# Expert weights loaded matrix by matrix in 16 KB runs, and the token gather cut into two halves of the slots

## The chip, the cores and the metric

The kernel runs on one core of one Trainium2 chip. The metric is the time of one execution on the device in microseconds (us), the median of several runs. A profile is one such execution, recorded by the hardware profiler. The work is spread over TensorE (PE in the rows, its weight loads PEld), VectorE (DVE), ScalarE (ACT), GpSimd (POOL) and SyncE (SP), which here only issues DMAs; 16 DMA engines carry them out.

## The reference

One decoder layer over 256 tokens of width 2048, all in float32. It ends in a mixture of 32 experts with 256 hidden columns each; every token uses 2 experts of one group.

```python
def hybrid_layer(x, ...):
    h = rms_norm(x, norm1_g)
    z = h @ w_in                                  # 2048 x 11272
    ...                                           # conv, mLSTM heads, attention heads, gates
    y = sigmoid(gm) * (hm @ w_branch_m) + sigmoid(ga) * (ha @ w_branch_a)
    x = x + y @ w_out
    x = x + hier_moe(rms_norm(x, norm2_g), ...)
    return x                                      # then a final RMSNorm

def hier_moe(h, w_grp, b_grp, w_exp, b_exp, w1, w3, w2):
    ...                                           # top group, top 2 experts in it, weights `combine`
    hid = silu(einsum('td,edf->tef', t, w1)) * einsum('td,edf->tef', t, w3)
    hid = hid * combine[..., None]
    return einsum('tef,efd->td', hid, w2)
```

Each expert has three matrices of 2 MiB (w1, w3, w2), so the experts read 201.3 MB; everything before them reads about 133 MB.

## The kernel before, in words

**Dense stages.** All matrices up to `w_out` stream through four buffers `wraw` of 1 MiB, are split by ACT and DVE into a rounded part and a rest (`wsplit`) and multiplied on PE. This part is the same in both kernels, but for one copy.

**From the router to the first expert (the seam).** After the last unit of `w_out` PE sums the router logits. DVE picks the two experts of every token, gives each of the 512 (token, expert) pairs a slot sorted by expert, and writes `sel`, a 0/1 matrix from the tokens to the 512 slots (L1613, L1616). PE gathers (L1081): for each of the 16 chunks of the width it multiplies the token rows, as a rounded part `x2hi` and a rest `x2lo`, by `sel`: four matmuls with 512 moving columns, their weights read with a step of 16 elements. A 17th product (L1078) gives each slot the RMS factor of its token. ACT and DVE in turn copy the chunks from PSUM to `xg`.

**Pairs of experts.** The experts are worked off two at a time, 16 pairs, with 64 slots each (an `If` chooses this form when no expert has more than 64 tokens; this run takes it). For each expert of a pair DVE multiplies the slots' columns of `xg` by the RMS factors into `xe`; PE multiplies `xe` by w1 and w3 side by side (`hidden`, L1094); ACT takes the sigmoid and DVE the products (`silu`); PE turns the result (`turn`). Then come the rows of w2 for both experts (`rows`, L1123), ACT and DVE split the sums into `ys_hi` and `ys_lo`, and PE spreads them to the tokens (`scatter`, L1139 and L1140, in eight groups of 512 columns), which DVE adds to `x2` (L1697). The scatter of a pair lies between the matmuls of the next.

**Buffers and loads.** `w13_a` and `w13_b` hold w1 and w3 of the even and the odd expert of one pair (4 MiB each). `w2s` has two slots of two buffers of 2 MiB, so the rows of two pairs. SP issues the loads in program order and waits before each until PE has used what the buffer held:

```python
def load_hidden(b, e, kh):                    # w1 and w3, one half of the contraction
    ks = slice(kh * HALF_K, (kh + 1) * HALF_K)
    for w, w_v in enumerate((w1_v, w3_v)):
        sp.dma_start(w13[b][:, kh, w], w_v[:, e, ks]).then_inc(w13_loaded[b][kh], 16)
```

Such a load has 8 KB in one run on each partition; a load of w2 has two runs of 4 KB. Before the gather ends, both `w13` and three of the four w2 buffers are filled; the fourth (`w2_a0`) shares its memory with `x2lo` and is loaded after the gather.

**The end.** After the last pair's rows the eight groups are scattered, added, squared on ACT and multiplied by `final_g` on DVE (L1742); then come the sum of squares, its root (POOL), the scaling and the store.

Of the kernel before, what the change touches and what calls it, by code (L numbers as in the profile page):

```python
# [14 lines left out]
F32 = mybir.dt.float32  # L15
F32R = mybir.dt.float32r
# [36 lines left out]
WARM_ROUTE, WARM_SELECT = 20, 12  # L53
# [21 lines left out]
GROUPS_OUT = TT * D // 512  # L75
REV = 384
# [55 lines left out]
def layer(nc, x, norm1_g, w_in, conv_w, if_bias, mnorm_g, w_branch_m, w_branch_a, w_out, rel_bias,  # L132
          norm2_g, w_grp, b_grp, w_exp, b_exp, w1, w3, w2, final_g, onehot, out):
    ctx = ExitStack()
    with ctx:
# [11 lines left out]
        def sem(name):  # L147
# [31 lines left out]
        x2hi = sb("x2hi", [P, TT, D], F32R, at=AT_QK + 16 * KB)  # L179
# [99 lines left out]
        hid = sb("hid", [P, P])  # L279
        sg = sb("sg", [P, P])  # L280
        spare = sb("spare", [P, 1])
        slot_w = sb("slot_w", [P, 1])
        mix = sb("mix", [P, TT, P])
        assert place["at"] <= AT_W2

        slot_of = sb("slot_of", [P, T], F32R, at=AT_ONES_R)
        hidT = sb("hidT", [P, 2, P], at=AT_IOTA_S)
# [40 lines left out]
        gexp_go, gexp_done, mk_ready, rank_summed, sel_ready, xg_summed, xg_act, xg_dve, tab_ready = (  # L328
            sem(n) for n in ("group_exp_go", "group_exp_done", "chosen_ready", "rank_summed",
                             "selection_ready", "gathered", "gathered_even", "gathered_odd",  # L330
                             "table_ready"))
        w13_loaded = [[sem(f"w13{b}_{kh}_loaded") for kh in ("upper", "lower")] for b in "ab"]
        w2_loaded = [[sem(f"w2_loaded{slot}_{side}") for side in ("left", "right")] for slot in range(2)]
        xe_ready, h_summed, sg_ready, hid_ready, hid_turned, hidT_ready, y_summed, ys_ready = (
            sem(n) for n in ("xe_ready", "hidden_summed", "hidden_sigmoid", "hid_ready", "hid_turned",
                             "hidT_ready", "ye_summed", "ye_ready"))
        upper_used = sem("upper_chunks_used")
# [16 lines left out]
        w2_v = w2.rearrange("e (j p) n -> p e j n", p=P)  # L354
# [9 lines left out]
        gathers = [*range(12), None, *range(12, DC)]  # L364
# [27 lines left out]
        def _(sp):  # L392
# [1385 lines left out]
```

## Time and profile before

| | before |
|---|---|
| time, median of 3 runs | 1253.61 us (1253.21 to 1253.68) |
| the profiled execution: time | 1249.93 us |
| its span | 1248.2 us |
| PE busy | 1193.2 us (96%) |
| DVE, ACT busy | 707.1 us (57%), 408.1 us (33%) |
| read from memory | 333.93 MB |
| core's mean DMA rate | 269 GB/s over the span |

The time is the device's for a whole execution, the span is from the first to the last recorded instruction, so the two differ by 1.7 us in the profiled execution. A busy PE isn't a PE at its peak, since matmuls overlap in the records: a high share says only that something is always in flight. The DMA share and the GB/s of a stretch say more about the last third of this kernel.

### The profile page before, as it was taken

What the parts mean: (1) busy time and instruction counts of PE and PEld (TensorE: products, weight loads), DVE (VectorE), ACT (ScalarE), POOL (GpSimd) and SP (SyncE); (2) the same over time, 40 slices, a digit from 0 to 9 for tenths busy, and PEclk for the clock granted to TensorE, in tenths of its full rate; (3) what the DMA queues carried; (4) which work ended last, traced back from release to release, by engine and by line L of the source; (5) the groups of instructions that cost most, each with busy time, mean ns of one, the idle gap of its engine ahead of it and who ended that gap; (6) DMA issues with size and microseconds to landing.
All of it is one profiled execution on the core that took longest, in us unless ns stands there. A gap on an engine that the chain in (4) does not pass through costs nothing.

```text
span 1248.2 us, 19400 instructions
## 1 busy us (share of the span) xinstructions
PE 1193.2 (96%) x7310; PEld 895.4 (72%) x7310; DVE 707.1 (57%) x1009; ACT 408.1 (33%) x464; POOL 38.3 (3%) x54
## 2 busy tenths in 40 slices
PE   8999999999999999999999998999999998999995
PEld 8888888888888888888888887555555544444442
DVE  5777555554666766667885555344454444444445
ACT  5444433334344354444344542111112111111113
POOL 1000000001002022000000000000000000000000
PEclk9999999999999999999999999999999999999997
DMA  8665655555555455556765674999999999999993
GB/s 286 191 188 183 186 184 182 189 180 176 183 169 170 136 166 168 168 168 192 248 177 172 236 304 149 366 417 424 425 426 425 425 425 426 424 425 425 425 424 151
DMA packets 170150, 336.57 MB, mean 270 GB/s; under 512 B 12144, under 2 KB 136192, under 8 KB 153088
## 3 DMA queue, kind: packets, MB, share of 16 engines
q1 hardware_dynamic: 165536, 335.69, 73.0%
q10 hardware_dynamic: 4576, 0.37, 0.3%
q8 instruction: 25, 0.41, 0.1%
q14 instruction: 13, 0.11, 0.0%
HBM read 333.93 MB, written 2.11 MB: 269 GB/s over the span
## 4 chain that ended last, share of the span: by engine, by line
PE 57%; issue 40%; DVE 1%; DMA 1%; ACT 0%; POOL 0%; ACTq 0%; POOLq 0%; SPq 0%; DVEq 0%
PE ps L836 19%; PE ps L865 11%; PE ps L838 10%; PE ps L867 5%; PE ps L1003 5%; PE ps L1004 2%; PE ps L823 1%; DMA xin<-in_x_dram 1%; PE ps L972 0%; PE ps L1023 0%; DVE wsplit L1188 0%; PE ps L852 0%; ACT wsplit L585 0%; PE ps L854 0%; PE ps L853 0%
## 5 line engine op out<-in xcount | busy, mean ns | idle before, releaser
L1188 DVE TENSOR_TENSOR wsplit<-wraw,wsplit 128x2048 fp32r<-128x2048 f32 x120 | 277.1, 2309 | 181.2 <-ACT wsplit L585 180.3
L836 PE MATMUL ps<-act_split,wsplit 128*128 128x512 f32 x1024 | 362.4, 399 | 0.0
L585 ACT ACTIVATE wsplit<-wraw 128x2048 fp32r<-128x2048 f32 x120 | 230.1, 1917 | 383.4 <-PE ps L838 203.4
L838 PE MATMUL ps<-act_split,wsplit 128*128 128x256 f32 x1024 | 286.8, 280 | 0.0
L836 PEld LDWEIGHTS ps<-act_split,wsplit 128*128 128x128 f32 x1024 | 192.2, 188 | 48.0 <-issue 1.8
L865 PE MATMUL ps<-wsplit,act_split 128*128 128x512 f32 x608 | 216.2, 400 | 2.2 <-DVE wsplit L1188 2.1
L838 PEld LDWEIGHTS ps<-act_split,wsplit 128*128 128x128 f32 x1024 | 193.3, 189 | 0.2
L867 PE MATMUL ps<-wsplit,act_split 128*128 128x256 f32 x608 | 170.3, 280 | 0.0
L865 PEld LDWEIGHTS ps<-wsplit,act_split 128*128 128x128 f32 x608 | 114.2, 188 | 30.9 <-issue 2.7
L1094 PE MATMUL ps<-w_a,xe 128*64 128x256 f32 x1024 | 115.4, 381 | 13.6 <-DMA w_a<-in_w_dram 11.4
L1672 DVE TENSOR_TENSOR hid<-sg,ps 128x128 f32<-128x128 f32 x32 | 9.2, 288 | 204.8 <-ACT sg L778 204.8
L1094 PEld LDWEIGHTS ps<-w_a,xe 128*64 128x64 f32 x1024 | 72.6, 137 | 61.3 <-DMA w_a<-in_w_dram 20.2
L1094 PE MATMUL ps<-w_b,xe 128*64 128x256 f32 x1024 | 115.7, 381 | 0.0
L867 PEld LDWEIGHTS ps<-wsplit,act_split 128*128 128x128 f32 x608 | 114.8, 189 | 0.0
L1123 PE MATMUL ps<-w_a,hidT 128*64 128x512 f32 x256 | 113.3, 595 | 0.4 <-ACT hidT L781 0.4
L1123 PE MATMUL ps<-w_b,hidT 128*64 128x512 f32 x256 | 113.3, 595 | 0.0
L1094 PEld LDWEIGHTS ps<-w_b,xe 128*64 128x64 f32 x1024 | 71.4, 137 | 41.6 <-issue 4.3
L1697 DVE TENSOR_TENSOR x<-x,ps 128x512 f32<-128x512 f32 x128 | 84.9, 683 | 8.9 <-PE ps L1140 6.9
L1003 PE MATMUL ps<-br_split,wsplit 128*128 128x512 f32 x256 | 88.8, 394 | 0.0
L1123 PEld LDWEIGHTS ps<-w_a,hidT 128*64 128x64 f32 x256 | 33.7, 137 | 70.0 <-issue 69.5
L1139 PE MATMUL ps<-ys_hi,slot_of 128*128 128x512 f32 x128 | 61.5, 480 | 18.5 <-DVE x L1697 18.5
L778 ACT ACTIVATE sg<-ps 128x128 f32<-128x128 f32 x32 | 8.9, 278 | 197.3 <-PE ps L1094 197.3
(288 smaller groups left out, 1148.3 us busy)
## 6 DMA issues: line engine op xcount, KB each, us to landing
w_a<-in_w_dram SPq DMA_DIRECT2D x96, 1024.0 KB, 18.4
w_b<-in_w_dram SPq DMA_DIRECT2D x96, 1024.0 KB, 21.5
wraw<-in_w_in_dram SPq DMA_DIRECT2D x88, 1024.0 KB, 5.0
wraw<-in_w_out_dram SPq DMA_DIRECT2D x16, 1024.0 KB, 5.2
wraw<-in_w_branch_m_dram SPq DMA_DIRECT2D x8, 1024.0 KB, 5.1
wraw<-in_w_branch_a_dram SPq DMA_DIRECT2D x8, 1024.0 KB, 5.1
xin<-in_x_dram SPq DMA_DIRECT2D x2, 1024.0 KB, 6.1
x<-in_x_dram SPq DMA_DIRECT2D x1, 2048.0 KB, 9.3
```

The source lines that it names most:

```text
L585: act.activation(wsplit[:, q % 2, :, 0], wraw[:, q % RAW], ACT.Copy).then_inc(rounded, 1)
L836: pe.matmul(banks[b], w[:, k, 0, b * P:(b + 1) * P], a, start=first and k == 0, stop=False)
L838: last = pe.matmul(banks[b][:, 0:T], w[:, k, 1, b * P:(b + 1) * P], a[:, 0], start=False, stop=last_half and k == HALF_K - 1)
L865: pe.matmul(banks[t], a[:, 0, t * P:(t + 1) * P], w[:, k], start=first and k == 0, stop=False)
L867: last = pe.matmul(banks[t][:, 0:UNIT], a[:, 1, t * P:(t + 1) * P], w[:, k, 0], start=False, stop=last_half and k == HALF_K - 1)
L1003: pe.matmul(bank, w[:, k, 0, b * P:(b + 1) * P], a, start=k == 0, stop=False)
L1004: last = pe.matmul(bank[:, 0:T], w[:, k, 1, b * P:(b + 1) * P], a[:, 0], start=False, stop=k == HALF_K - 1)
L1094: last = pe.matmul(ps[f * SLOTS:(f + 1) * SLOTS, 0, 0:2 * P].rearrange("p (w f) -> p w f", w=2), xe[:, b, k], w13[b][:, k // HALF_K, :, k ...
L1123: last = pe.matmul(ps[b * SLOTS:(b + 1) * SLOTS, 2 + n], hidT[:, b, f * SLOTS:(f + 1) * SLOTS], w2s[slot][b][:, f, n * 512:(n + 1) * 512], ...
L1139: pe.matmul(ps[:, 6 + g % 2], to_tokens, ys_hi[:, n * 512:(n + 1) * 512], start=True, stop=False)
L1188: dve.tensor_tensor(wsplit[:, q % 2, :, 1], wraw[:, q % RAW], wsplit[:, q % 2, :, 0].bitcast(F32), ALU.subtract).then_inc(split, 1)
L1697: dve.tensor_tensor(cols, cols, ps[:, 6 + g % 2], ALU.add).then_inc(added, 1)
```

## The change

Four things change, all from the seam on.

1. **Loads.** w1 and w3 of an expert are loaded as whole matrices (2 MiB, one run of 16 KB on each partition), w1 of both experts once the pair before has used w1, then w3 likewise. w2 is cut as `(p j)` in place of `(j p)`, so that it too has one run of 16 KB. The first pairs are loaded in parts of 1 MiB (8 KB runs), the last pair's w2 in pieces of 512 columns. `w2_a0` moves to memory that is free early and is loaded ahead of the gather.
2. **Order in a pair.** PE multiplies by w1 for both experts, then by w3 for both, in four parts; one `turn` for the pair; two scatter groups of the pair before stand behind each part. The RMS factor and the routing weight are applied to the hidden values, so `xe` is a plain copy.
3. **Gather.** It runs over the first 256 slots (`side` 0) and then over the other 256 (`side` 1), each with 16 chunks of four matmuls with 256 moving columns. Eleven chunks of side 0 stand ahead of the first pair, the rest between its parts. ACT alone copies to `xg`. `x2` is made again from `x2hi` + `x2lo` after the gather.
4. **Tail.** The last pair's rows, rounding, scatter, adds and squares go piece by piece; POOL multiplies six groups by `final_g`, DVE two.

```diff
-            def load_hidden(b, e, kh):
-                ks = slice(kh * HALF_K, (kh + 1) * HALF_K)
-                for w, w_v in enumerate((w1_v, w3_v)):
-                    sp.dma_start(w13[b][:, kh, w], w_v[:, e, ks]).then_inc(w13_loaded[b][kh], 16)
+                def next_hidden(i):
+                    for w, w_v in enumerate((w1_v, w3_v)):
+                        parts_done(i, 2 * w + 1)
+                        for b in range(2):
+                            sp.dma_start(w13[b][:, w], w_v[:, ds(i * 2 + b, 1)]).then_inc(w13_loaded[w][0], 16)
+                def next_rows(i, slot):
+                    rows_free(i)
+                    for b in range(2):
+                        load_rows(slot, b, ds(i * 2 + b, 1))
...
-        w2_v = w2.rearrange("e (j p) n -> p e j n", p=P)
+        w2_v = w2.rearrange("e (p j) n -> p e j n", p=P)
...
+            def gather(side, first, end):
+                pe.wait_ge(sel_ready, side + 1)
+                for c in range(first, end):
+                    n = side * DC + c
+                    if n >= 5:
+                        pe.wait_ge(xg_out, n - 4)
+                    for t in range(TT):
+                        for k, part in enumerate(parts):
+                            last = pe.matmul(ps[:, 3 + n % 5, 0:SIDE], part[:, t, c], sel[:, t, side * SIDE:(side + 1) * SIDE],
+                                             start=t == 0 and k == 0, stop=t == TT - 1 and k == 1)
+                    last.then_inc(xg_summed, 1)
+            gather(0, 0, AHEAD)
...
+                for part in range(PARTS):
+                    w, h = divmod(part, 2)
...
+                    for k in range(h * PART_K, (h + 1) * PART_K):
+                        for b in range(2):
+                            last = pe.matmul(ps[b * SLOTS:(b + 1) * SLOTS, 2 * w, 0:FF], operands[b][:, k], w13[b][:, w, k],
+                                             start=k == 0, stop=k == DC - 1)
+                    last.then_inc(h_parts, 1)
...
+                hidden(0, 0, (xg[:, :, 0:SLOTS], xe_first), [[lambda: gather(0, AHEAD, DC)], [lambda: gather(1, 0, 6)],
+                                                             [lambda: gather(1, 6, 12)], [lambda: gather(1, 12, DC)]])
+                turn(0)
+                pe.wait_ge(xg_out, 2 * DC)
+                rows(0, 0, 0)
...
+                    hidden(i, i, xe, [[lambda: scatter(i - 1, half, (0, 1))], [lambda: scatter(i - 1, half, (2, 3))],
+                                      [lambda: scatter(i - 1, half, (4, 5))], [lambda: scatter(i - 1, half, (6, 7))]])
+                    turn(i)
```

Where DVE makes `sel`, this stood in the kernel before (engine DVE; `table`, `rank` and `pos` are the slot counts, `ps` is PSUM):

```order
L1602 COPY table<-ps 128x32
L1603 SCALAR_TENSOR_TENSOR table<-ones,ps 128x31
L1605 COPY rank<-ps 128x64
L1607 TENSOR_TENSOR pos<-rank,table 128x64
L1609 TENSOR_TENSOR rt<-oh,pos 128x64 x2
L1611 TENSOR_REDUCE stat<-rt 128x4
L1613 TENSOR_SCALAR sel<-iota_s,stat 128x512 x2
L1616 SCALAR_TENSOR_TENSOR sel<-iota_s,stat,sel 128x512 x2
```

And this stands there now, on the same engine:

```order
L1718 SCALAR_TENSOR_TENSOR table<-ones,ps 128x31
L1721 TENSOR_TENSOR pos<-ps,table 128x64
L1723 TENSOR_TENSOR rt<-oh,pos 128x64 x2
L1725 TENSOR_REDUCE stat<-rt 128x4
L1731 TENSOR_SCALAR sel<-iota_s,stat 128x256 x2
L1735 SCALAR_TENSOR_TENSOR sel<-iota_s,stat,sel 128x256 x2
L1740 COPY rank<-ps 128x64
L1741 COPY table<-ps 128x32
```

Two small copies moved behind `sel`, and `sel` is made for 256 slots at first; the other 256 come after the first pair's tokens were copied.

On PE, the end of the gather and the first pair stood like this before (two matmuls of the last chunk, the branch into the pair-wise form, then the first pair):

```order
L1081 MATMUL ps<-sel,x2hi 128x512
L1081 MATMUL ps<-sel,x2lo 128x512
L369 TENSOR_LOAD most_i
L369 ISA x2
L370 COMPARE_AND_BRANCH
L1094 MATMUL ps<-w_a,xe 64x256 x32
L1112 MATMUL ps<-ident,hid 128x128
L1094 MATMUL ps<-w_b,xe 64x256 x32
L1109 MATMUL ps<-ident,mix 128x128 x2
```

Now, at the end of the first pair's first part, PE's rows are these (the last two of 16 matmuls of the part, the turn of `mix`, and the first two matmuls of the gather's next five chunks):

```order
L1186 MATMUL ps<-w_a,xg 64x256
L1186 MATMUL ps<-w_b,xe_first 64x256
L1167 MATMUL ps<-ident,mix 128x128 x2
L1155 MATMUL ps<-sel,x2hi 128x256
L1155 MATMUL ps<-sel,x2lo 128x256
```

A gather matmul is half as wide and there are 128 of them in place of 64; 44 stand ahead of the first pair, 20, 24, 24 and 16 behind its four parts, and all of them stand ahead of the pair's rows.

On SP, one turn of the loop loaded this for a pair before (`w_a` and `w_b` are the buffers of the even and the odd expert, ISA rows are waits and register work):

```order
L448 DMA w_a<-in_w_dram 128x2048 x2
L480 REGISTER_ALU
L448 ISA
L448 DMA w_a<-in_w_dram 128x2048 x2
L448 ISA
L448 DMA w_b<-in_w_dram 128x2048 x2
L480 REGISTER_ALU
L448 ISA
L448 DMA w_b<-in_w_dram 128x2048 x2
L489 REGISTER_ALU
L454 DMA w_a_61<-in_w_dram 128x2x1024
L454 DMA w_b_62<-in_w_dram 128x2x1024
```

And now:

```order
L492 DMA w_a<-in_w_dram 128x4096
L492 ISA
L492 DMA w_b<-in_w_dram 128x4096
L485 REGISTER_ALU
L492 DMA w_a<-in_w_dram 128x4096
L492 DMA w_b<-in_w_dram 128x4096
L464 ISA
L464 DMA w_a_63<-in_w_dram 128x4096
L464 ISA
L464 DMA w_b_64<-in_w_dram 128x4096
```

Six loads of 2 MiB take the place of twelve of 1 MiB; SP waits three times a pair, each wait ahead of 4 MiB, where it waited five times.

## Rows read from the trace of the kernel before

**Rows 1.** The page's slices: DMA share in tenths, GB/s, 40 slices of 31.2 us

```profile
DMA  8665655555555455556765674999999999999993
GB/s 286 191 188 183 186 184 182 189 180 176 183 169 170 136 166 168 168 168 192 248 177 172 236 304 149 366 417 424 425 426 425 425 425 426 424 425 425 425 424 151
```

**Rows 2.** Windows: length, busy us (x count) by engine, PE clock, DMA share, GB/s

```profile
757.00:774.00 17.00, 16.10 (x65) 14.88 (x64) 7.88 (x19) 6.12 (x9) 0.00 (x0) 1.00 0.17 67
774.00:782.00 8.00, 6.75 (x63) 4.51 (x64) 3.23 (x6) 1.49 (x2) 0.00 (x0) 1.00 0.91 298
803.00:806.00 3.00, 3.00 (x30) 2.01 (x28) 0.00 (x0) 0.00 (x0) 0.00 (x0) 1.00 0.54 137
850.00:1000.00 150.00, 144.07 (x990) 78.23 (x986) 69.28 (x119) 28.12 (x45) 0.00 (x0) 1.00 1.02 425
1222.00:1223.00 1.00, 1.00 (x6) 0.29 (x4) 0.00 (x0) 0.00 (x0) 0.00 (x0) 1.00 0.68 287
```

**Rows 3.** Windows: w2 loads (4 KB runs), then w1 and w3 (8 KB runs)

```profile
1001.50:1011.30 9.80, 9.32 (x73) 5.58 (x72) 2.45 (x5) 0.55 (x2) 0.00 (x0) 1.00 1.01 418
1011.50:1031.00 19.50, 17.39 (x109) 8.29 (x107) 10.10 (x17) 4.27 (x6) 0.00 (x0) 1.00 1.02 428
```

**Rows 4.** Timeline of the seam: start, length, engine, line, what, count

```profile
753.47 0.88 DVE L1613 TENSOR_SCALAR sel<-iota_s,stat 128x512 fp32r<-128x512 f32 x2
754.39 1.41 DVE L1616 SCALAR_TENSOR_TENSOR sel<-iota_s,stat,sel 128x512 fp32r<-128x512 f32 x2
...
759.60 0.30 PEld L1081 LDWEIGHTS ps<-sel,x2hi 128*128 128x128 f32 x1
759.84 0.30 PEld L1081 LDWEIGHTS ps<-sel,x2lo 128*128 128x128 f32 x1
...
772.71 0.39 PE L1081 MATMUL ps<-sel,x2lo 128*128 128x512 f32 x1
...
775.25 7.13 PE L1094 MATMUL ps<-w_a,xe 128*64 128x256 f32 x64 [2.15 <-DVE xe L1658]
...
792.65 0.64 PE L1123 MATMUL ps<-w_a,hidT 128*64 128x512 f32 x1 [0.37 <-ACT hidT L781]
...
799.57 7.08 PE L1094 MATMUL ps<-w_a,xe 128*64 128x256 f32 x64
...
803.40 4.32 SPq L448 DMA_DIRECT2D w_a<-in_w_dram  x4
```

**Rows 5.** Timeline of the last dense unit: weight loads without a step

```profile
738.70 0.19 PEld L852 LDWEIGHTS ps<-wsplit,act_split 128*128 128x128 f32 x1
738.82 0.19 PEld L853 LDWEIGHTS ps<-wsplit,act_split 128*128 128x128 f32 x1
```

**Rows 6.** SP's DMA issues, the first load of two pairs that follow each other

```profile
830.79 4.25 SPq L448 DMA_DIRECT2D w_a<-in_w_dram  x4
...
858.18 4.24 SPq L448 DMA_DIRECT2D w_a<-in_w_dram  x4
```

**Rows 7.** Timeline: two scatter groups, and the turn ahead of the rows

```profile
1206.27 0.50 PE L1139 MATMUL ps<-ys_hi,slot_of 128*128 128x512 f32 x1
...
1207.07 0.40 PE L1140 MATMUL ps<-ys_lo_left,slot_of 128*128 128x512 f32 x1
...
791.96 0.33 PE L1112 MATMUL ps<-ident,hid 128*128 128x128 f32 x1 [0.65 <-DVE hid L1673]
```

**Rows 8.** The tail: timeline rows, then groups of instructions (count, busy us, mean ns)

```profile
1219.96 0.64 PE L1123 MATMUL ps<-w_a,hidT 128*64 128x512 f32 x1
...
1239.04 0.15 DVE L1747 TENSOR_REDUCE stat<-sq 128x2 f32<-128x8 f32 x1
...
L1697 DVE TENSOR_TENSOR x<-x,ps 128x512 f32<-128x512 f32 x128 | 84.9, 683 | 8.9 <-PE ps L1140 6.9
L786 ACT ACTIVATE ys_hi<-ps,slot_w 128x1024 fp32r<-128x1024 f32 x32 | 35.7, 1114 | 108.4 <-PE ps L1123 108.4
L794 ACT ACTIVATE fin<-x 128x512 f32<-128x512 f32 x8 | 5.0, 630 | 4.8 <-DVE x L1697 4.8
```

More of the change, by code:

```diff
@@ L1065, in _ @@
             last.then_inc(rank_summed, 1)
+            pe.wait_ge(rms_diag_ready, 1)
+            for t in range(TT):
+                last = pe.matmul(ps[:, 2, t * P:(t + 1) * P], ones[:], rms_diag[:, t], start=True, stop=True)
+            last.then_inc(rms_summed, 1)
             for n in range(WARM_SELECT):
@@ new lines, in turn, with rows @@
+            def turn(s):
+                pe.wait_ge(hid_ready, s + 2)
+                pe.wait_ge(hidT_ready, s + 1)
+                pe.wait_ge(slots_ready, s + 2)
+                for f in range(FC):
+                    last = pe.transpose(ps[:, 1, f * P:(f + 1) * P], hid[:, f * P:(f + 1) * P], ident[:])
+                last.then_inc(hid_turned, 1)
+            def rows(load_no, s, slot, ns=range(4)):
+                pe.wait_ge(hidT_ready, s + 2)
+                pe.wait_ge(ys_ready, s * 2 + 1)
+                if load_no is not None:
+                    pe.wait_ge(w2_loaded[slot], load_no * 32 + 32)
+                for n in ns:
+                    if load_no is None:
+                        pe.wait_ge(w2_last[n], 32)
@@ new lines, in experts, with pair @@
+                copy_rms_row()
+                second_tokens(0)
+                make_mix(0, 0, 0)
+                select(1)
+                second_tokens(1)
+                dve.memset(xg[:, :, PAIRS:], 0.0)
+                slots(0, 0)
+                gate(0)
+                up(0)
+                make_x2()
+                dve.wait_ge(xg_out, 2 * DC)
+                copy_tokens(starts_of(1, 0), 1)
+                make_mix(1, 0, 1)
+                def pair(i, half):
+                    ys_split(i - 1)
+                    slots(i, half, (i - 1) * GROUPS_OUT + 1)
+                    add(i - 1, (0, 1, 2, 3))
+                    gate(i)
+                    add(i - 1, (4, 5))
+                    up(i)
+                    add(i - 1, (6, 7))
@@ new lines, in experts @@
+                with steps_x.loop(0, N_PAIRS // 2 - 1, 4) as j:
+                    for n in (1, 2):
+                        i = j * 2 + n
+                        pair(i, n % 2)
+                        copy_tokens(starts_of(i + 1, 0), i + 1)
+                        make_mix(i + 1, 0, i + 1)
+                pair(LAST, 1)
+                for n in range(4):
+                    ys_split_part(LAST * 2 + (n + 1), n, n + 1)
+                    tail_add((2 * n, 2 * n + 1))
+            by_most(dve, experts)
```

515 lines of the change are left out of this document (282 added, 233 removed).

## The prediction

> **What bounds the kernel now.** I read the page's slices first. In the dense stages the DMA engines are busy half to two thirds of the time; from the 27th slice on they are busy throughout at 424 to 426 GB/s, up to the last slice [rows 1]. The stretch from 850 to 1000 us says it at one glance: share 1.02, 425 GB/s, PE's clock at its full 1.00 [rows 2]. So the pairs of experts are paced by the weights' arrival, not by PE. Then I looked for the edges of that stretch. Ahead of it is a hole: from 757 to 774 us the engines are busy 0.17 of the time, 774 to 782 runs at 298 GB/s, and at 803 to 806 there is a second, small hole (0.54, 137 GB/s) [rows 2]. At its end the stream stops in the slice 1222 to 1223, two thirds full, so at about 1223.1 [rows 2]; what comes behind is the tail, 25.1 us up to the span's end at 1248.2.
>
> The first hole's reason is room. All buffers but one are full, and SP may load again only when PE has used something: the gather ends at 772.71 + 0.39, the first pair's matmuls start at 775.25, its rows at 792.65, and the second pair starts at 799.57; the load that opens the unbroken stream is issued at 803.40 [rows 4]. At that point both experts' matrices of pairs 0 and 1, 12 of the 96 matrices of 2.097 MB, have been loaded. What is left is 84 of them and `final_g`, 176.2 + 1.05 = 177.2 MB. At 425 GB/s that takes 417.0 us; counted from 806, where the flow is back, it gives 1223.0, which is where the stream ends [rows 2]. So the end is: the moment at which the stream can start, plus bytes over rate, plus the tail. The change touches all three.
>
> **The start of the stream.** In the new order, SP has room for the first pair's parts during the seam: w1 and w3 of pair 1, the same 4 matrices as before. The next load, w2 of pair 2, waits for the rows of pair 0 to be done, and the bytes behind that point are again 84 matrices and `final_g`. So the new start of the stream is the end of the first pair's rows, where it was 803.40.
>
> - Making `sel`: DVE took 0.88 us for two instructions of 512 columns and 1.41 us for two more [rows 4]. With half the columns, and a fixed part that I put at 0.06 us in each (estimate, as the small DVE instructions of about 0.2 us bound it), they take 0.50 and 0.77, 1.0 less; a copy moved behind gives 0.1 more: **-1.1 us**.
> - The gather: before, from the end of `sel` at 755.80 to 773.10, it was 64 matmuls, 0.24 us apart (759.60 and 759.84), and the RMS product, some 17 us [rows 4]. Now it is 128 matmuls with half the moving columns. No row shows one. The bounds: a 256-column matmul whose weights lie side by side goes every 0.12 us (738.70 and 738.82) [rows 5], so 128 x 0.12 = 15.4 us; or the spacing stays at the 0.235 us of the 512-column ones, 30.1 us. What decides is the weight load: with the step of 16 elements it takes 0.30 us, without it 0.19 [rows 4, 5]. If the 0.11 us more is time in which the load occupies its path, the spacing can't go below 0.12 + 0.11 = 0.23, and halving the columns halves nothing. I take 0.23: 29.5 us, **+12.5 us**.
> - The waits: between the gather's end and the first rows there were 792.65 - 773.10 = 19.55 us, of which 2 x 7.13 = 14.3 were matmuls of `hidden` [rows 4] (the second expert's group is as long) and 5.3 were waits for `xe` and for the two silu chains. Now the silu of the gate lies under the gather, and what is left is the turn of `mix` (0.4), the wait of the second part for the 16th chunk's copy and the token copy (0.9), and a turn with the copy of `hidT` ahead of the rows (0.69 before, 791.96 to 792.65 [rows 7, 4], for two transposes 0.85). With 0.5 for the branch, which is no longer under a wait, 2.65: **-2.7 us**. The rows stay at 6.9 us.
>
> Together +8.7: the rows of pair 0 end at 799.57 + 8.7 = 808.3, and the stream's first load is issued at 808.4, **5.0 us later than 803.40**. `make_x2` (two DVE instructions) and the token copies of pair 1 lie under the rows; without that cover they would cost up to 5 us. The extra 2 MiB that is loaded ahead finds room between 740 and 760 us and buys nothing by itself, since the w2 buffer it fills was already refilled before 803 in the kernel before.
>
> A rule bears on the gather. The Trainium skill, page "SBUF — State Buffer", section "Specifications (TRN2)", says that an engine's reads run at full bandwidth only with at least two hits in a 16-byte line. Four-byte elements with a step of 16 never give that, and the trace agrees: 0.30 against 0.19 us. By that rule the gather takes the 29.5 us; without it 15.4.
>
> **Bytes over rate.** The two kinds of load can be told apart in the trace: while w2 comes (4 KB runs) 418 GB/s, while w1 and w3 come (8 KB runs) 428 [rows 3]. Each of 16 engines then needs 156.8 ns for 4 KB and 306.2 ns for 8 KB: 149.4 ns for each 4 KB, and 7.4 ns that come with the run whatever its length. A 16 KB run should take 306.2 + 298.8 = 605 ns, which is 433 GB/s. The lower bound for the rate is the 428 of the 8 KB runs, or the 425 of today if w2's other layout explains nothing. 82 of the 84 matrices, 172.0 MB, take 397.2 us at 433 and took 404.6 at 425: **-7.4 us**. The last two w2 come in runs of 2 KB: 82.1 ns each, 399 GB/s, 10.5 us for 4.19 MB where it was 9.9: **+0.6 us**.
>
> The Trainium skill, page "DMA: Bandwidth & Descriptors", section "Bandwidth", gives 435 GB/s as the ceiling of the fabric and about three cycles on top of each packet. By an estimate from that page the 16 KB runs reach 432, so 6.5 us would be gained in place of 7.4.
>
> So the stream ends at 1223.1 + 5.0 - 7.4 + 0.6 = 1221.3.
>
> **The tail.** Before, rows to sum of squares took 1239.04 - 1219.96 = 19.1 us [rows 8], and the rows started 3.1 us ahead of the stream's end. Now the last w3 is in flight until 1221.3 - 2.5 - 10.5 (`final_g` and w2 stand behind it) + 1.5 for its arrival to be seen (estimate: the last pair's PE work before stood about as far behind the stream) = 1209.8. PE then does two parts of 3.6 us, two scatter pairs of 1.05 (1206.27 to 1207.07 and one spacing of 0.24 more [rows 7]), the turn and the wait for `hidT` (1.2): rows start at 1220.4. The rest goes piece by piece. PE: 1.7 us of rows per piece, so 6.9 in all, and three scatter pairs between them, 3.2. Behind the last piece: rounding 0.6 (half of 1114 ns, and a little), split 0.7, scatter 1.1, two adds 1.4, the last square 0.8 [rows 8], and 0.7 for signals between engines: 15.4 us, to 1235.8; and DVE's two products by `final_g` may push it by 0.5. Sum of squares at 1236.3, and 9.2 us from there to the end as before (1239.04 to 1248.2): 1245.5. The tail is 24.2 us behind the stream, against 25.1; with PE's clock, which I don't know there, I take **-1.3 us** with 1 us of doubt either way. POOL's products for six groups are at most 2 us each and end before the last square.
>
> **The sum**: 5.0 - 7.4 + 0.6 - 1.3 = -3.1 us. The span goes from 1248.2 to 1245.1, the profiled execution from 1249.93 to 1246.8; the median of the runs lies 3.7 above the profiled execution, which I carry over: **1250.5 us**. A difference of 0.2% (2.5 us) is about the least that a measurement of this kernel can tell from none, so this is barely a gain. Its own range is 1246 to 1256: the stream's start may be off by 2 us, the rate by 3, the tail by 1.5.
>
> **Rivals.**
>
> *The step in the weights costs nothing with fewer columns.* The 128 matmuls then go at 0.12 us: 14.1 us less than in my sum, everything behind follows, since the stream is unbroken. Time 1236. For it: the 0.30 us might be delay and not occupancy, for the loads overlap at 0.24 us spacing. Against it: the loads without a step keep 0.19 us at either spacing, so the length of a record does look like service. Chance 0.16.
>
> *The runs' length gives nothing.* Then the rate stays at 425 and the 7.4 us are missing: 1258; at 428, the present best, 4.6 us are missing: 1255. For it: the two rates come from windows of 10 and 20 us and differ by only 2.4%, and w2's pieces differ from the others also in where they lie in memory. Against it: the mean of 425 over 150 us [rows 2] is what one third at 418 and two thirds at 428 give, so the difference is not noise of these windows. Chance 0.14, most of it slower.
>
> *PE becomes the bound (the other side).* Loads are freed in steps of 4 MiB now. PE's own pace before was 27.4 us a pair, while it still had a lead of data (830.79 to 858.18) [rows 6]. I count 4 x 3.67 + 6.9 + 4 x 1.05 + 0.3 + 0.85 = 27.0 for the new order: the scatter in pairs meets free banks, but `hidT` is waited for in the open. The stream needs 12.58 MB / 433 = 29.1 us a pair. PE starts pair 1 at 808.3 and must be at the second half of pair 15 at 1209.8; that is 14 periods and 9.8 us, so it decides above 28.0 us a pair, with 14 us for each further 1 us. At 28.5 the time is 1257.5. Against it: the margin of 1 us; DVE has some 14 us of work in a pair, and each of SP's waits ends 3 to 10 us before the stream would run dry. Chance 0.13, nearly all slower.
>
> What is left, 0.05, is a tail or a seam that is shorter in some way I don't see (0.04), or longer.
>
> **How the numbers follow.** Mine 0.52 (0.32 faster by over 0.2%, 0.18 within, 0.02 slower), the free step 0.16 (faster), no gain in rate 0.14 (0.04 within, 0.10 slower), PE as the bound 0.13 (0.02, 0.11), the rest 0.05 (0.04 faster, 0.01 slower): faster 0.52, same 0.24, slower 0.24. The range takes in 1236 of the first rival and 1258 of the second.
>
> **What would show it.** In the changed kernel: gather matmuls with 256 columns at a spacing near 0.23 us (or 0.12, then the first rival); the rows of pair 0 ending near 808; slices of the pairs at 432 to 434 GB/s; PE waiting for the DMA at w1 and w3 in the later pairs, and pairs 29 us apart; the stream ending near 1221 and the sum of squares 15 us behind it. The prediction is wrong if the stream runs dry between pairs, if the rate stays at 425, or if the gather is cheap.

## The result, and the profile after

The changed kernel takes 1257.89 us (median of 5 runs, 1255.55 to 1259.0), the kernel before 1253.21 (5 runs on the same chip): ratio 1.0034, 95% interval 1.002 to 1.0048. It is slower by 0.34%, where 1250.5 us and a small gain were forecast. The profiled execution took 1255.84 us, its span 1254.0.

The page's slices answer to [rows 1]:

```profile
GB/s 285 191 185 187 194 174 194 173 198 171 176 164 166 156 162 164 166 163 191 266 176 171 253 351 187 221 428 430 432 431 432 432 430 432 430 432 432 408 390 115
```

The weights now come at 430 to 432 GB/s, up to the 37th slice. Then it falls to 408 and 390.

The timeline of the seam (start, length, engine, line, what), beside [rows 4]:

```profile
753.24 0.62 DVE L1731 TENSOR_SCALAR sel<-iota_s,stat 128x256 fp32r<-128x256 f32 x2
753.89 0.88 DVE L1735 SCALAR_TENSOR_TENSOR sel<-iota_s,stat,sel 128x256 fp32r<-128x256 f32 x2
...
755.31 0.31 PEld L1155 LDWEIGHTS ps<-sel,x2hi 128*128 128x128 f32 x1
755.44 0.38 PE L1155 MATMUL ps<-sel,x2hi 128*128 128x256 f32 x1
755.53 0.31 PEld L1155 LDWEIGHTS ps<-sel,x2lo 128*128 128x128 f32 x1
755.66 0.38 PE L1155 MATMUL ps<-sel,x2lo 128*128 128x256 f32 x1
...
801.12 0.61 PE L1213 MATMUL ps<-w_a,hidT 128*64 128x512 f32 x1 [0.67 <-ACT xg L806]
808.01 0.38 PE L1186 MATMUL ps<-w_a,xe_a 128*64 128x256 f32 x1
808.24 0.33 SPq L464 DMA_DIRECT2D w_a<-in_w_dram  x1
```

The gather's matmuls of 256 columns are 0.22 us apart, pair 1 starts at 808.01, and SP issues the load that opens the stream at 808.24 (forecast 808.4). The same timeline has the gather's 128 matmuls in five stretches that fill 29.4 us of PE (forecast 29.5), with 2.4 us of waits between the gather's start and the rows (forecast 2.65).

The timeline of PE at the heads of two steady pairs and of the last two, with the wait ahead of each in brackets; SP's issue of w1 of pair 15; the third part of pair 15 (the first that needs its w3, 1218.62); the last rows; and DVE's sum of squares:

```profile
1065.22 0.43 PE L1186 MATMUL ps<-w_a,xe_a 128*64 128x256 f32 x1 [1.87 <-DMA w_b<-in_w_dram]
...
1094.35 0.43 PE L1186 MATMUL ps<-w_a,xe_a 128*64 128x256 f32 x1 [1.89 <-DMA w_b<-in_w_dram]
...
1181.91 0.43 PE L1186 MATMUL ps<-w_a,xe_a 128*64 128x256 f32 x1 [1.90 <-DMA w_b<-in_w_dram]
...
1190.53 0.33 SPq L492 DMA_DIRECT2D w_a<-in_w_dram  x1
...
1209.01 0.38 PE L1186 MATMUL ps<-w_a,xe_a 128*64 128x256 f32 x1
...
1218.62 0.43 PE L1186 MATMUL ps<-w_a,xe_a 128*64 128x256 f32 x1
...
1228.87 0.64 PE L1213 MATMUL ps<-w_a,hidT 128*64 128x512 f32 x1 [0.47 <-ACT hidT L821]
...
1244.32 0.15 DVE L1922 TENSOR_REDUCE stat<-sq 128x2 f32<-128x8 f32 x1
```

A steady pair takes 29.13 us (1065.22 to 1094.35), and once in it PE waits 1.9 us for w1. The last such wait is at 1181.91, for w1 of pair 14. From there on PE waits for no load, w3 of pair 15 included: pair 14 takes 27.1 us, pair 15 another 19.9 up to its rows. The last rows start at 1228.87, 8.5 us later than forecast [rows 8 for before].

The windows there say that the stream was no longer the one that set the pace (the last three numbers are PE's granted clock, where 1.00 is its full level, the DMA share and GB/s):

```profile
1180.00:1188.00 8.00, 6.10 (x51) 3.88 (x52) 3.10 (x8) 1.02 (x1) 0.00 (x0) 1.00 1.02 436
1188.00:1194.00 6.00, 6.00 (x50) 3.69 (x48) 2.35 (x5) 0.47 (x1) 0.00 (x0) 1.00 0.69 240
1194.00:1202.00 8.00, 7.33 (x54) 4.41 (x50) 3.22 (x5) 0.38 (x1) 0.00 (x0) 1.00 1.01 426
1202.00:1206.00 4.00, 3.90 (x18) 1.39 (x20) 2.19 (x6) 0.15 (x1) 0.00 (x0) 1.00 0.97 307
1206.00:1226.00 20.00, 20.00 (x150) 11.65 (x148) 7.87 (x14) 2.38 (x3) 0.00 (x0) 1.00 1.01 406
```

At 1188 to 1194 the engines run at 240 GB/s while PE is busy in all 6 us. SP issues w1 of pair 15 at 1190.53, when PE has used w1 of pair 14; here w2 of pair 15 stood in between before. A second, smaller hole follows at 1202 to 1206 (307 GB/s), ahead of w3 of pair 15, for the same reason.

### The profile page after: what moved, and what is told of

It is laid out like the page before. It is cut to its first block, busy times and chain, and to the rows that moved or that the text cites. A ratio compares the mean times of both kernels' runs of the same rounds, so it can differ in the third digit from the quotient of the medians.

```text
span 1254.0 us, 19144 instructions
## 1 busy us (share of the span) xinstructions
PE 1199.7 (96%) x7366; PEld 909.2 (73%) x7366; DVE 693.0 (55%) x1019; ACT 383.6 (31%) x419; POOL 45.8 (4%) x60
## 4 chain that ended last, share of the span: by engine, by line
PE 77%; DMA 18%; DVE 2%; issue 1%; ACT 1%; SPq 0%; POOL 0%; ACTq 0%; POOLq 0%; DVEq 0%
PE ps L904 19%; DMA w_b<-in_w_dram 17%; PE ps L1186 12%; PE ps L933 11%; PE ps L906 10%; PE ps L935 5%; PE ps L1071 5%; PE ps L1213 3%; PE ps L1072 2%; PE ps L1155 2%; PE ps L1222 1%; PE ps L1223 1%; DMA xin<-in_x_dram 1%; PE ps L891 1%; PE ps L1091 1%
## 5 line engine op out<-in xcount | busy, mean ns | idle before, releaser
L1186 PE MATMUL ps<-w_a,xe_a 128*64 128x256 f32 x960 | 219.8, 382 | 19.9 <-DMA w_b<-in_w_dram 19.7
L1186 PE MATMUL ps<-w_b,xe_b 128*64 128x256 f32 x960 | 219.8, 382 | 0.0
L1186 PEld LDWEIGHTS ps<-w_a,xe_a 128*64 128x64 f32 x960 | 126.9, 137 | 109.0 <-DMA w_b<-in_w_dram 34.3
L1186 PEld LDWEIGHTS ps<-w_b,xe_b 128*64 128x64 f32 x960 | 126.9, 137 | 0.0
L1837 DVE TENSOR_TENSOR x<-x,ps 128x512 f32<-128x512 f32 x120 | 77.1, 684 | 84.9 <-PE ps L1223 81.6
L1072 PE MATMUL ps<-br_split,wsplit 128*128 128x256 f32 x256 | 70.9, 277 | 0.0
L827 ACT ACTIVATE ys_hi<-ps 128x1024 fp32r<-128x1024 f32 (+1 forms) x34 | 33.1, 973 | 98.7 <-PE ps L1213 98.7
L1222 PE MATMUL ps<-ys_hi,slot_of 128*128 128x512 f32 x128 | 56.9, 445 | 1.5 <-DVE ys_lo_right L1822 1.5
```

What stands on the lines that cost most here:

```text
L1072: last = pe.matmul(bank[:, 0:T], w[:, k, 1, b * P:(b + 1) * P], a[:, 0], start=False, stop=k == HALF_K - 1)
L1186: last = pe.matmul(ps[b * SLOTS:(b + 1) * SLOTS, 2 * w, 0:FF], operands[b][:, k], w13[b][:, w, k], start=k == 0, stop=k == DC - 1)
L1222: pe.matmul(ps[:, bank], to_tokens, ys_hi[:, n * 512:(n + 1) * 512], start=True, stop=False)
L1837: dve.tensor_tensor(cols, cols, ps[:, 6 + g % 2], ALU.add).then_inc(added, 1)
```

## The experiments

The profiled executions differ by up to 6 us in when `sel` starts (751.6 to 757.7 us), although all kernels but the one before share nearly all of the code up to there; the changed kernel's own two differ by 1.7 us. So I read each run in three stretches: from the first row of `sel` to the head of pair 1 (the seam), from there to the first row of the last pair's `rows` (the stream), and from there to the sum of squares (the tail).

| kernel | `sel` starts | seam | stream | tail | time or ratio |
|---|---|---|---|---|---|
| before | 753.47 | 46.1 | 420.4 | 19.1 | 1 |
| changed | 753.24 | 54.8 | 420.9 | 15.5 | 1.0034 |
| changed, forecast | | 54.8 | 412.1 | 15.9 | |
| one_gather | 756.91 | 43.0 | 421.5 | 15.5 | 0.9922 |
| w2_lag_early | 755.67 | 54.8 | 418.0 | 15.5 | 1.0019 |
| no_last_w2 | 755.07 | 54.8 | 421.0 | 15.5 | 1257.68 us |
| pad_last | 754.23 | 54.8 | 424.4 | 15.5 | 1260.31 us |
| one_gather_lag_early | 755.40 | 43.0 | 417.0 | 15.5 | 0.9921 |
| gather_side_by_side | 755.51 | 41.6 | 420.7 | 15.4 | 1244.67 us |
| short_runs | 753.37 | 56.4 | 422.1 | 15.5 | 1258.81 us |
| pad_every_pair | 757.71 | 54.8 | 425.2 | 15.5 | 1264.65 us |
| changed_again | 751.55 | 54.8 | 420.5 | 15.5 | 1.0036 |
| w2_in_place | 755.43 | 54.8 | 425.3 | 15.5 | 1.0063 |

The three stretches are the same to 0.4 us in both profiles of the changed kernel, so differences of a microsecond count in them, even where one execution's time could not tell them. One thing has to be taken out first: in some executions the granted clock falls to its lower level (0.50 in the rows, 1.2 GHz in place of 2.4) for 3.4 to 6.8 us in the midst of the work. Where PE sets the pace, 3.4 us of it cost 1.7. The seam of short_runs and the streams of w2_lag_early and w2_in_place have one such stretch each that PE has to pay for. From the sum of squares to the span's end the changed kernel takes 9.7 us, 0.5 more than before; that lies in the store, and I did not follow it up.

The forecast missed in the stream alone, by 8.8 us.

My theory after the result: behind the arrival of w1 of pair 14 stand 47 us of PE's own work, and the stream, with w2 of pair 15 moved to its end, no longer covers them. The rivals: the stream ended too late, by its holes and the pieces of 2 KB runs; or PE bound the whole way.

**no_last_w2.** The changed kernel without the loads of the last pair's w2 and the waits for them (the rows of pair 15 are made with what is in the buffer):

```
                 cols = slice(n * 512, (n + 1) * 512)
-                for b in range(2):
-                    sp.dma_start(w2s[1][b][:, :, cols], w2_v[:, 2 * LAST + b, :, cols]).then_inc(w2_last[n], 16)
...
-                    if load_no is None:
-                        pe.wait_ge(w2_last[n], 32)
```

> The changed kernel without the loads of the last pair's w2 and the waits for them; the last pair uses the rows of pair 13 that are in the buffer, so this part of the result is left out. The stream ends 10 us earlier. Theory A (PE gates the end): the last rows start at 1228 to 1229 as before and the span stays within 1 us of 1254.0. Rival B (the stream's end decides): the span falls by 8 to 10 us.

The stream stretch is 421.0 against 420.9, although 4.2 MB less are loaded at its end. PE's rows at the last head and the last rows:

```profile
1210.97 0.38 PE L1184 MATMUL ps<-w_a,xe_a 128*64 128x256 f32 x1
...
1230.81 0.64 PE L1209 MATMUL ps<-w_a,hidT 128*64 128x512 f32 x1 [0.47 <-ACT hidT L819]
```

Again 19.84 us between them. The span, 1256.0, is 1 us outside what I had expected; `sel` starts 1.8 us later here. The stream's late end costs nothing; PE sets the end.

**pad_last.** 16 matmuls of `ident` more, behind the third part of the last pair, into a bank that the rows overwrite:

```
+                def pad():
+                    for _ in range(16):
+                        pe.matmul(ps[:, 5, 0:P], ident[:], ident[:], start=True, stop=True)
...
-                                        [lambda: scatter(LAST - 1, 0, (4, 5))], [lambda: scatter(LAST - 1, 0, (6, 7))]])
+                                        [lambda: scatter(LAST - 1, 0, (4, 5)), pad], [lambda: scatter(LAST - 1, 0, (6, 7))]])
```

> The changed kernel with 16 matmuls of the identity (32 records of 0.12 us, 3.8 us) added behind the third part of the last pair. Theory A (PE gates the end): the span grows by 3.8 us, all of it. Rival B (PE waits for the last w2 pieces or w3 there): the span grows by 0 to 1 us.

```profile
1210.01 0.38 PE L1186 MATMUL ps<-w_a,xe_a 128*64 128x256 f32 x1
...
1233.41 0.64 PE L1213 MATMUL ps<-w_a,hidT 128*64 128x512 f32 x1 [0.47 <-ACT hidT L821]
```

23.4 in place of 19.9 us, 3.5 more. The added matmuls run from 1224.25 to 1227.9, so all of their time is paid (it is 3.5 and not the 3.8 that I had counted). Nothing else is waited for in the last pair.

**pad_every_pair.** The same with 8 matmuls, in pairs 1 to 15 (in `hidden_and_scatter`).

> 8 more matmuls of 128 columns behind the third part of every pair from 1 to 15, 1.7 us by the run with 16 of them. Theory (PE has slack of 1.9 us in each pair from 4 to 13, and none in 14 and 15): the last rows start 3.4 us later counted from the start of pair 1, 424.3, and the time is about 1261 us; the wait for w_b in the steady pairs falls from 1.9 us to 0.2. Rival (the prediction's third rival, PE decides from 28.0 us a pair on, 14 us for each further 1 us): PE's own pace is now 28.7, so 0.7 x 14 = 10 us are to be paid, 1268 us; if PE bound every pair, 15 x 1.7 = 25 us.

```profile
1158.00 0.43 PE L1186 MATMUL ps<-w_a,xe_a 128*64 128x256 f32 x1
...
1187.22 0.43 PE L1186 MATMUL ps<-w_a,xe_a 128*64 128x256 f32 x1
1216.07 0.38 PE L1186 MATMUL ps<-w_a,xe_a 128*64 128x256 f32 x1
...
1237.68 0.64 PE L1213 MATMUL ps<-w_a,hidT 128*64 128x512 f32 x1 [0.47 <-ACT hidT L821]
```

The pairs are 28.8 us apart (1187.22 to 1216.07) but for the one before, 29.2 (1158.00 to 1187.22), and at no head does PE wait for a load longer than 0.1 us, where I had expected 0.2. Yet pair 14 starts 374.7 us behind pair 1, against 373.9 without the padding. So in the first 13 pairs 13 x 1.75 us were swallowed but for 0.8, and the last two paid 1.8 each: +4.3, where I expected 3.4 and the rival 10 or 25. The time of 1264.65 us also holds a `sel` that started 4.5 us late. The limit from which PE sets the start of pair 14 is 373.9 / 13 = 28.8 us a pair; PE's own pace is 27.0. PE did not bind the whole way.

**w2_in_place.** The last w2 stands again between w3 of pair 14 and w1 of pair 15, `final_g` at the end:

```
                 next_hidden(LAST - 1)
-                next_hidden(LAST)
                 rows_free(LAST)
                 for n in range(4):
-                    if n == 0 and chunks == 1:
-                        load_final_g(chunks)
...
+                next_hidden(LAST)
+                load_final_g(chunks)
```

> The last pair's w2 is loaded in its old place, between w3 of pair 14 and w1 of pair 15; final_g comes last. Theory (behind w1 of pair 14 stand 27.1 us of PE for pair 14 and 20 for pair 15, and without the last w2 only 3 matrices of 9.7 us in the stream): with w2 back there PE waits for w1 and then w3 of pair 15, and the last w3 sets the end. The stream has no hole near 1190 and ends near 1223; w3 is there near 1221.5, and two parts, two scatter pairs and the turn (10.4 us) bring the last rows to 1232, 3 us later than 1228.9, 424 us behind the start of pair 1: about 1260 us. So w2 at the end is worth 3 us of the 10.8 that the prediction booked for it. Rival (the late place costs by the hole in the stream, which then ends later): without the hole everything ends 2.7 us earlier, 1255 us.

```profile
1184.14 0.43 PE L1183 MATMUL ps<-w_a,xe_a 128*64 128x256 f32 x1 [1.91 <-DMA w_b<-in_w_dram]
...
1213.96 0.40 PE L1183 MATMUL ps<-w_a,xe_a 128*64 128x256 f32 x1 [2.49 <-DMA w_b<-in_w_dram]
...
1235.53 0.64 PE L1210 MATMUL ps<-w_a,hidT 128*64 128x512 f32 x1 [0.47 <-ACT hidT L818]
```

PE waits again for w1 of pair 15 (2.5 us). From that head to the rows it takes 21.6 us in place of 19.9, but not by a wait for w3, as I had expected: the only waits there are the 2.5 us at the head and the 0.47 for `hidT`. It is the clock. Just behind the wait the granted clock falls to its lower level, and the matmuls of the first part go every 0.43 us in place of 0.22:

```profile
1214.90:1218.30 3.40, 3.40 (x20) 2.38 (x18) 0.00 (x0) 0.00 (x0) 0.00 (x0) 0.50 1.00 424
```

The stretch is 425.3, 4.4 longer than with w2 last; 1.7 of them are the clock, 2.7 the order (3 expected). And the time is 1261.5 us, ratio 1.0063 [1.0047, 1.008] against 1.0036 [1.0023, 1.0048] for the changed kernel on the same chip. The hole at 1188 is nearly gone (401 GB/s), and it is no faster: the hole wasn't the cause. Moving w2 to the end is right, and worth some 3 us in the stretch (4 in the medians, 1261.5 and 1257.36), not the 10.5 by which it was to bring w3 forward.

**changed_again**, beside it.

> The changed kernel again, on the same chip as the next one: 1256 to 1259 us, the last rows 421 us behind the start of pair 1.

1257.36 us (6 runs), stream stretch 420.5.

**w2_lag_early.** If PE's 47 us behind w1 of pair 14 set the end, w1 must come earlier in the stream, and something else later. Up to pair 10 w2 is loaded a pair ahead of its w1; here w2 of pair 11 and of those that follow goes behind w1 and w3 of the same pair:

```
-                with sp.Fori(0, N_PAIRS // 2 - 2) as j:
+                with sp.Fori(0, N_PAIRS // 2 - 4) as j:
...
-                next_hidden(LAST - 1)
+                next_hidden(LAST - 5)
+                for i in range(LAST - 4, LAST):
+                    next_hidden(i)
+                    next_rows(i, i % 2)
                 next_hidden(LAST)
```

> The changed kernel with w2 of a pair moved behind its w1 and w3 from pair 11 on, and not for the last pair alone. Theory A (PE gates the end: from the arrival of w1 of pair 14 it has 27.1 us of pair 14 and 20 us of pair 15 to do before the last rows, where the stream needs only 29.1 us for the three loads between): the hole in the stream moves to 1070-1080 us and stays 2 to 3 us long, PE has caught up by the end, the last rows start 3.5 to 4.5 us earlier than 1228.8, the time falls by as much, to about 1254. Rival B (the stream's own end or its holes decide): no change within 1 us, or 1 to 3 us slower.

```profile
1067.44 0.43 PE L1189 MATMUL ps<-w_a,xe_a 128*64 128x256 f32 x1 [1.88 <-DMA w_b<-in_w_dram]
1094.53 0.38 PE L1189 MATMUL ps<-w_a,xe_a 128*64 128x256 f32 x1
...
1177.56 0.43 PE L1189 MATMUL ps<-w_a,xe_a 128*64 128x256 f32 x1 [1.84 <-DMA w_b<-in_w_dram]
...
1206.85 0.40 PE L1189 MATMUL ps<-w_a,xe_a 128*64 128x256 f32 x1 [1.96 <-DMA w_b<-in_w_dram]
...
1228.42 0.64 PE L1216 MATMUL ps<-w_a,hidT 128*64 128x512 f32 x1 [0.47 <-ACT hidT L824]
```

Three pairs run at PE's own 27.0 us. Pair 14 starts 367.1 us behind pair 1, 6.8 earlier. But pair 14 takes 29.3 us, since PE now waits for w1 of pair 15 (1.96 us), and pair 15 takes 21.6 up to its rows in place of 19.9, so 2.9 are left: 418.0. The 1.7 us in pair 15 are no wait. They are a stretch at the lower clock, again just behind the wait:

```profile
1208.10:1211.50 3.40, 3.40 (x20) 2.45 (x17) 0.00 (x0) 0.00 (x0) 0.00 (x0) 0.50 1.01 429
```

Ratio 1.0019 [1.0007, 1.0031]. That is the direction the theory asks for, but the intervals of the two kernels overlap; only the trace tells the 2.9 us.

**gather_side_by_side.** The gather takes 128 neighbouring channels as weights, in place of every 16th (the channels come out in another order than the reference's, so this is a measurement and not a kernel to use):

```
-            parts = [part[:].rearrange("p t (q c) -> p t c q", c=DC) for part in (x2hi, x2lo)]
+            parts = [part[:].rearrange("p t (c q) -> p t c q", c=DC) for part in (x2hi, x2lo)]
```

> The gather takes 128 channels that lie side by side as weights, in place of every 16th, with the same count of matmuls and columns; the channels then come out in another order than the reference's. Theory (the step in the weights makes the load long and the load sets the spacing): weight loads fall from 0.30-0.32 to 0.19 us, matmuls go every 0.12 us where nothing else holds them, and ACT's copies (some 0.45 us for a chunk of 4 matmuls, 0.48 us) are then about as slow, so the gather loses 10 to 14 us and the start of pair 1 moves from 808 to 795-799 us; about 1245 us in all. Rival (the spacing of 0.22 us is that of a matmul with 256 columns in this program, whatever the weights): spacing and start stay, 1257 us.

The group of weight loads, then two matmuls:

```profile
L1155 PEld LDWEIGHTS ps<-sel,x2hi x64: 186/192/193, 757.2 to 788.8; 128*128 128x128 f32 x64
...
757.50 0.28 PE L1155 MATMUL ps<-sel,x2hi 128*128 128x256 f32 x1
757.62 0.28 PE L1155 MATMUL ps<-sel,x2lo 128*128 128x256 f32 x1
```

The loads take 0.192 us in place of 0.316, the matmuls go every 0.12 us in place of 0.22, and the seam is 13.1 us shorter. The step in the weights is what the gather's second half costs.

**one_gather.** The gather in one group of 512 columns again, before pair 0's second part, everything else as changed:

```
-SIDE = 256
+SIDE = 512
...
-                hidden(0, 0, (xg[:, :, 0:SLOTS], xe_first), [[lambda: gather(0, AHEAD, DC)], [lambda: gather(1, 0, 6)],
-                                                             [lambda: gather(1, 6, 12)], [lambda: gather(1, 12, DC)]])
+                hidden(0, 0, (xg[:, :, 0:SLOTS], xe_first), [[lambda: gather(0, AHEAD, DC)], [], [], []])
                 turn(0)
-                pe.wait_ge(xg_out, 2 * DC)
+                pe.wait_ge(xg_out, DC)
```

> The changed kernel with the gather in one piece again: SIDE is 512, so 16 chunks of four matmuls with 512 moving columns, 11 ahead of the first pair, 5 behind its first part. Theory A (the strided weight loads hold each gather matmul at 0.22 us whatever its width, and the seam is paid in full because the stream behind it is unbroken): the gather takes 64 x 0.235 = 15 us in place of 28.2, sel 0.9 more, so SP issues the first w2 load near 796 us in place of 808.24 and the time falls by 12 us against the changed kernel, to about 1246. Rival B (PE is what gates the end, and it has its slack elsewhere, so the seam's length is partly absorbed): the load comes at 796 but the time falls by less than 6 us.

1243.87 us (1242.26 to 1247.79), ratio 0.9922 [0.9905, 0.9938]. The seam is 43.0 us, 11.7 less than changed (12 expected) and 3.1 less than before; the stream is 0.6 longer. These 0.6 us lie ahead of pair 4, where PE waits for a load for the first time: 1.57 us there, 0.93 in the changed kernel. The windows around the head of pair 1, of one_gather (head at 799.94) and then of the changed kernel (808.01), offer a reason: here the engines still carry the loads ahead of the stream when it is to open, there they have nothing to do:

```profile
799.00:803.00 4.00, 4.00 (x36) 2.80 (x33) 3.30 (x7) 1.02 (x1) 0.00 (x0) 1.00 0.89 322
...
805.00:808.00 3.00, 3.00 (x16) 1.18 (x14) 1.82 (x5) 0.92 (x1) 0.00 (x0) 1.00 0.00 0
```

The halves of the gather alone turn a gain of 0.8% into a loss.

**one_gather_lag_early.** Both edits.

> The gather in one group of 512 columns, and the loads of w2 going over to the later place at pair 11. Theory: the two edits act at different ends and add up. The one gather gave 1243.87 us; the early change of places took 2.9 us off the last pair's rows, counted from the start of pair 1, and about 2 off the time: 1241 to 1242 us, ratio 0.990 to 0.992, last rows 418 us behind the start of pair 1. Rival: the stream's end takes over as the gate (the last rows can't start much before the last w3 is there and two parts, two scatter pairs and the turn are done, 10.4 us), then nothing is added and it stays at 1243.9.

The slices: the hole has moved to the 35th, where PE has a lead to spend, and the last full one stays at 425:

```profile
GB/s 286 195 185 188 180 193 172 195 176 171 199 158 162 159 169 169 146 164 199 229 211 180 179 409 139 334 429 430 431 431 431 431 431 431 381 431 431 431 425 164
```

1242.41 us (1241.12 to 1244.82, 5 runs), ratio 0.9921 [0.9907, 0.9934]: 0.8% ahead of before and the fastest here by its median. The stream stretch fell to 417.0. Against one_gather the ratio tells no difference; the trace shows 4.5 us in this stretch, more than the 2.9 of w2_lag_early, since no stretch at the lower clock falls into pair 15 here (19.84 us up to the rows). That the two edits add up is shown by the trace, not by the times.

**short_runs.** w1 and w3 in two loads with half the rows each, w2 with one row a run; order and bytes as changed:

```
-        w2_v = w2.rearrange("e (p j) n -> p e j n", p=P)
+        w2_v = w2.rearrange("e (j p) n -> p e j n", p=P)
...
-                            sp.dma_start(w13[b][:, w], w_v[:, ds(i * 2 + b, 1)]).then_inc(w13_loaded[w][0], 16)
+                            for h in range(2):
+                                ks = slice(h * PART_K, (h + 1) * PART_K)
+                                sp.dma_start(w13[b][:, w, ks], w_v[:, ds(i * 2 + b, 1), ks]).then_inc(w13_loaded[w][h], 16)
```

> w1 and w3 come in two loads of half the rows each (8 KB runs in place of 16 KB) and w2 in 4 KB runs, the order and the bytes the same. Theory (run length sets the rate): the slices fall from 431 to 424-426 GB/s, pairs are 29.5-29.6 us apart in place of 29.15, and the last rows start some 5 to 6 us later, 426 us behind the start of pair 1: about 1262 us. Rival (the length of the runs gives nothing, the rate came from whole matrices one after another): 431 GB/s and 1257 us.

The expectation had one size wrong: a whole row of w2 is 8 KB, so this kernel has 8 KB runs throughout (they are 4 KB in before because a load takes half of the columns there). The page, and the window from 870 to 1000 us of this kernel:

```profile
DMA packets 163081, 336.60 MB, mean 268 GB/s; under 512 B 11728, under 2 KB 135776, under 8 KB 138336
...
870.00:1000.00 130.00, 120.73 (x820) 66.08 (x816) 52.41 (x101) 12.13 (x18) 0.00 (x0) 0.99 1.01 428
```

The same window of the changed kernel:

```profile
870.00:1000.00 130.00, 119.75 (x814) 64.70 (x812) 54.58 (x103) 12.47 (x18) 0.00 (x0) 1.00 1.01 431
```

428 GB/s is what the 8 KB runs had in [rows 3]. So the gain from 425 has two halves: whole rows of w2, 4 KB to 8 KB, give 425 to 428; whole matrices, 8 KB to 16 KB, give 428 to 431. Neither theory as I wrote it held (424 to 426, or 431), but the first one's mechanism did. The w2 of an expert is one load of 2 MiB in both kernels, and from 850 to 1150 us one lands on average 4.90 us behind the load before it here, 4.86 in the changed kernel: 428 and 431 GB/s. So it is the run and not the size of the load.

The stream stretch is only 1.2 us longer, which understates the rate: w1 comes in two loads here, and PE can start on the first halves. Counted from the start of pair 1, PE starts pair 14 at 375.0 us (373.9 in the changed kernel), while the whole of its w1 lands at 377.4 (373.9). The seam is 1.6 us longer by the clock, which stands at its lower level in the first pair:

```profile
774.60:778.00 3.40, 3.31 (x16) 2.17 (x18) 2.01 (x6) 1.29 (x2) 0.00 (x0) 0.50 0.22 92
```

## Why the prediction was wrong, by its steps

- **The start of the stream** was right, and not by luck: the seam is 54.8 us, as forecast, and so are its parts within 0.3 (gather 29.4 for 29.5, waits 2.4 for 2.65). The step makes the load 0.316 us, the spacing 0.22 (0.23 taken, which is right with the changes of part counted in), and halving the columns halves nothing; without the step it is 0.12. The first rival, which had the step for free, is dead. The rule of the Trainium skill that the prediction weighed there (page "SBUF — State Buffer", section "Specifications (TRN2)") is borne out by both sides: 0.316 with the step, 0.192 without. The waits saved (2.7 forecast) show nearly alone in one_gather: its seam is 3.1 us shorter than before.
- **Bytes over rate** was right in kind and 1.4 us too large. 172.0 MB at 431.5 GB/s are 398.6 us, against 404.6: -6.0 in place of -7.4. The second rival, no gain from the runs' length, falls with short_runs. By the estimate from the Trainium skill (page "DMA: Bandwidth & Descriptors", section "Bandwidth") it was 432; the measured 431 to 432 lies a little nearer to that than to my 433, but a difference of 1 GB/s decides nothing here.
- **The tail term is the step that failed.** The prediction gates the last pair by the arrival of its w3, at 1209.8, and puts the rows 10.6 us behind it. In that sum it never asked when PE would be there. w3 of pair 15 was to arrive early only because w2, 10.5 us of stream, no longer stands ahead of it; behind w1 of pair 14 the stream then has three loads of 9.7 us, while PE has 27.1 + 19.9 = 47.0 us of work. On record, w1 of pair 14 comes at 1221.3 - 2.5 - 10.5 - 3 x 9.7 + 1.5 = 1180.7, so 372.4 us behind the start of pair 1, and the rows 412.1: 39.7 us for what takes 47.0. That is 7.3 of the 8.8 us; the other 1.5 are the later arrival of w1 of pair 14 (373.9 for 372.4), about what the lower rate makes. In the trace PE reaches the third part of pair 15, the first that needs w3, at 1218.62, without a wait. From the rows to the sum of squares the forecast held: 15.5 for 15.9. (Its own terms gave -0.9 for the tail; the -1.3 that it booked had no further reason.)
- **The stream's end** was 1226.4 (385 GB/s from 1224 to 1226, 119 in the microsecond behind), not 1221.3. That is an effect: SP may not issue w1 of pair 15 before PE has used w1 of pair 14. no_last_w2 shows that it costs nothing. The prediction had named the sign itself: it is wrong "if the stream runs dry between pairs", and it runs dry at 1188 to 1194 and at 1202 to 1206.
- **The third rival, PE as the bound,** had the right engine and the wrong place. PE's pace is 27.0 us a pair, as counted. It was judged as a mean over 14 periods with a limit of 28.0. But the pairs from 4 on are paced by the stream for as long as PE waits in each, and only what PE does behind its last wait counts: there 27.0 us a pair are paid in full, however far that lies below 29.1. The rival's condition, "above 28.0", was false, and its result, slower, came all the same.
- **The median**: I carried over 3.7 us between the profiled execution and the median; it was 2.1. Counted from `sel` to the span's end the forecast was 9 us too low, in the median 7.4, so 1.6 us of the miss are hidden there by luck.

In sum: the seam loses 8.7 us and the rate gives 6.0. Of the gain in rate and order, 7.3 us never come, since the last two pairs are PE's; so the stretch from pair 1 to the last rows is 420.9 us, against 420.4 before, and the tail, 3.6 shorter, cannot pay for the seam.

What shifts the start of `sel` by up to 6 us goes with the clock for the larger part. In the four profiles with no stretch at the lower clock ahead of `sel` it starts at 751.6 to 753.5 us; in the other eight, with 3.4 to 13.6 us at the lower clock, at 754.2 to 757.7, the latest in pad_every_pair, which has the 13.6. Here is the stretch of 6.8 us in one_gather:

```profile
746.30:753.10 6.80, 6.77 (x31) 6.77 (x32) 4.23 (x23) 2.65 (x7) 0.00 (x0) 0.50 0.58 233
```

If each of these stretches costs half its length, as in pair 15 (an estimate), the spread of 6.2 us shrinks to 2.9. Left open are the rest, why the clock falls in one execution and not in another of nearly the same kernel, and the 0.5 us in the store.

## What to carry to other kernels

When a load is moved to the end of a stream, find the last wait of the computing engine for an earlier load and add up that engine's own work behind it; a pace that is covered in every steady round is bare in the last ones. Count a split matmul by its weight load: where weights are read with a step, half the columns with twice the matmuls cost nearly twice the time here. And line up executions at an event ahead of the change before microseconds are compared, and look at the granted clock of a stretch before a longer one is put down to a wait.

## What the hardware showed that I had not expected

- The rate still rises beyond 8 KB runs: 425 GB/s for the mix of 4 and 8 KB, 428 for 8 KB, 431 to 432 for 16 KB, and 408 where w2 comes in 2 KB runs (1217 to 1224 us of the changed kernel):

```profile
1217.00:1224.00 7.00, 7.00 (x52) 4.13 (x50) 2.62 (x5) 0.47 (x1) 0.00 (x0) 1.00 1.05 408
```

- A weight load of 128 x 128 with a step of 16 elements takes 0.316 us, and the matmul spacing with 256 columns is 0.22; side by side 0.192 and 0.12. At 512 columns the matmuls with the step go every 0.24 us [rows 4], and those of the scatter, whose loads take 0.19, every 0.23: the step costs next to nothing there, presumably since the columns cover it.
- A wait can cost more than its length. In the changed kernel PE waits 1.9 us for w1 in each of ten pairs, and its clock stays at 1.00 through all of them. In w2_lag_early and w2_in_place the clock falls to 0.50 right behind waits of 1.96 and 2.49 us, for 3.4 us, in which the matmuls go every 0.43 us in place of 0.22; that costs 1.7 us. In one_gather_lag_early a wait of 1.95 us is followed by no such fall. No run here shows what decides between them.
